# Splitting one memory value panel over four steps of an attention loop instead of two (one core)

## The reference, cut to what matters

```python
def memory_cross_attn(x, memn, wq, wkv, wo):
    B, S, _ = x.shape
    Mm = memn.shape[1]
    q = (x @ wq).reshape(B, S, XA_HEADS, XA_DH)
    k, v = jnp.split(memn @ wkv, 2, axis=-1)
    k = k.reshape(B, Mm, XA_HEADS, XA_DH)
    v = v.reshape(B, Mm, XA_HEADS, XA_DH)
    s = jnp.einsum('bshd,bmhd->bhsm', q, k).astype(jnp.float32) * (XA_DH ** -0.5)
    p = jax.nn.softmax(s, axis=-1)
    o = jnp.einsum('bhsm,bmhd->bshd', p.astype(v.dtype), v).reshape(B, S, XA_HEADS * XA_DH)
    return o @ wo
```

## Time and profile before

| | |
|---|---|
| median of 3 runs | 1854.23 us (1853.72 to 1860.33) |
| profiled execution | 1850.81 us |
| its span, first to last instruction | 1849.0 us |
| mean granted TensorE clock | 0.981 |
| busy: PE, DVE, ACT, POOL | 96%, 57%, 20%, 10% |
| first attention steps of the change, layer 0 | from 904 us |
| the same, layer 1 | from 1431 us |

### The profile page before, as it was taken

The page is one execution under the profiler, slowest core; times in us unless marked ns, Lnnn a source line. Parts: engine busy times, 40 slices in busy tenths (PEclk is TensorE's granted clock), DMA queues, the critical chain, the costliest instruction groups (busy, mean ns, idle before and its releaser), DMA issues.

```text
span 1849.0 us, 22062 instructions
## 1 busy us (share of the span) xinstructions
PE 1768.0 (96%) x8510; PEld 1303.6 (71%) x8510; DVE 1052.9 (57%) x2078; ACT 361.3 (20%) x885; POOL 190.8 (10%) x126
## 2 busy tenths in 40 slices
PE   7999999989899999999999999999999999999997
PEld 6886488644746886476785759994668776689953
DVE  6776565343654777561163048996812451369985
ACT  1111000140511111102261112220012340222210
POOL 1212111000020222111000100002110000000010
PEclk9999999989999999999989999999999899999999
DMA  9644364521164545346412525543455205164440
GB/s 327 198 147 172 115 223 137 203 69 68 47 200 149 178 166 182 114 136 177 168 47 83 178 71 180 183 160 136 156 140 187 89 1 188 63 200 154 171 159 23
DMA packets 162502, 265.59 MB, mean 144 GB/s; under 512 B 4008, under 2 KB 105684, under 8 KB 162270
## 3 DMA queue, kind: packets, MB, share of 16 engines
q1 hardware_dynamic: 157470, 248.18, 39.9%
q0 software_dynamic: 4768, 15.48, 2.5%
q10 hardware_dynamic: 160, 0.52, 0.1%
HBM read 262.56 MB, written 1.08 MB: 143 GB/s over the span
## 4 chain that ended last, share of the span: by engine, by line
PE 75%; DVE 15%; DVEq 4%; ACT 3%; issue 2%; DMA 1%; SPq 0%; ACTq 0%
PE psum L764 14%; PE psum L924 11%; PE psum L820 9%; PE psum L737 8%; PE psum L727 6%; PE psum L1042 4%; PE psum L1077 3%; PE psum L1303 3%; PE psum L1260 3%; PE psum L714 3%; DVE work L2296 3%; PE psum L975 2%; PE psum L876 2%; DVE ring L1813 2%; PE psum L862 2%
## 5 line engine op out<-in xcount | busy, mean ns | idle before, releaser
L608 POOL TENSOR_TENSOR work<-ring,work 128x1024 f32<-128x1024 f32 (+1 forms) x57 | 141.4, 2481 | 803.9 <-DVE work L1815 803.9
L924 PE MATMUL psum<-ring,work 128*128 128x512 f32 x352 | 161.1, 593 | 2.7 <-DVE work L2329 2.7
L1811 DVE TENSOR_TENSOR work<-ring 128x1024 f32<-128x1024 f32 (+1 forms) x83 | 102.2, 1232 | 80.1 <-PE psum L924 77.7
L737 PE MATMUL psum<-ring,x_t 128*128 128x512 f32 x320 | 140.0, 595 | 7.4 <-ACT x_t L1361 7.4
L924 PEld LDWEIGHTS psum<-ring,work 128*128 128x128 f32 x352 | 66.3, 190 | 84.3 <-issue 79.9
L924 PE MATMUL psum<-work 128*128 128x512 f32 x264 | 122.6, 593 | 0.1
L737 PEld LDWEIGHTS psum<-ring,x_t 128*128 128x128 f32 x320 | 60.0, 190 | 81.5 <-issue 71.8
L1955 DVE CUSTOM_DVE_ANT_0 work<-psum,work 128x256 f32<-128x256 f32 (+1 forms) x96 | 31.4, 364 | 140.6 <-PE psum L1042 140.5
L1813 DVE TENSOR_TENSOR ring<-ring 128x1024 f32<-128x1024 f32 (+1 forms) x83 | 102.3, 1232 | 6.2
L1815 DVE TENSOR_TENSOR work<-ring 128x1024 f32<-128x1024 f32 (+1 forms) x83 | 99.6, 1200 | 6.5 <-issue 0.4
L1042 PE MATMUL psum<-work 128*128 128x256 f32 (+2 forms) x416 | 90.0, 351 | 3.9 <-ACT work L1596 2.2
(11 more groups left out here) (253 smaller groups left out, 2933.5 us busy)
## 6 DMA issues: line engine op xcount, KB each, us to landing
ring<-in_ffn_w_up_dram SPq DMA_DIRECT2D x66, 1024.0 KB, 8.0
ring<-in_w_in_dram SPq DMA_DIRECT2D x21, 2048.0 KB, 7.9
ring<-in_ffn_w_down_dram SPq DMA_DIRECT2D x20, 2048.0 KB, 7.8
ring<-in_ffn_w_gate_dram SPq DMA_DIRECT2D x22, 1024.0 KB, 5.5
ring<-in_xa_wkv_dram SPq DMA_DIRECT2D x8, 2048.0 KB, 8.0
ring<-in_w_out_dram SPq DMA_DIRECT2D x6, 2048.0 KB, 8.7
ring<-in_xa_wq_dram SPq DMA_DIRECT2D x4, 2048.0 KB, 7.8
ring<-in_xa_wo_dram SPq DMA_DIRECT2D x4, 2048.0 KB, 9.5
```

The lines of the kernel that those rows point to most:

```text
L608: nc.gpsimd.tensor_tensor(t4, quarters(n, chunks, pitch)[2], t2, ALU.subtract).then_inc(fourth_ready, 1)
L737: return mm(bank(banks[2 * i + h]), acts[:, c, i * P:(i + 1) * P], ring[:, (n0 + c // 4) % RING, o:o + 512], start=(c == 0), stop=(c == KD ...
L924: last = mm(sums[p], acts[p][:, q, :], rhs[:, i, :], start=(q == 0), stop=(q == KF // 2 - 1))
L1811: v.tensor_tensor(t3, b22, b12, ALU.subtract)
```

## The change

The tile function gets a range of chunks. Each of four steps, 1 to 4, now computes one piece: tile 0 chunks 0 to 3, tile 0 chunks 4 to 7, tile 1 chunks 0 to 3, tile 1 chunks 4 to 7. The wait for the memory keys stays at step 1, now ahead of the first piece; the wait for the panel's arrival moves there too. `panel_done` is incremented behind the fourth piece. ACT copies at its step 5 instead of 4.

```diff
-                def memory_values(j, tiles, banks):
+                def memory_values(j, tiles, banks, chunks=range(KD)):
 
                     n = at(L_WV[j], N_LAYER, l)
-                    if 0 in tiles:
+                    if 0 in tiles and 0 in chunks:
                         arrived(n)
                     for i in tiles:
-                        for k in range(KD):
+                        for k in chunks:
                             last = mm(bank(banks[i]), MEMT[:, k, i * P:(i + 1) * P], ring[:, n % RING, k * 512:k * 512 + 512],
                                       start=(k == 0), stop=(k == KD - 1))
-                    if 1 in tiles:
+                    if 1 in tiles and KD - 1 in chunks:
                         last.then_inc(panel_done, 1)
 
-                def keys_out():
-                    pe.wait_ge(group_free, at(H_WK + 2, G_LAYER, l))
-
-                def first_values():
-                    memory_values(0, (0,), (1, 3))
-
-                def second_values():
-                    memory_values(0, (1,), (1, 3))
+                def values_between(i, half):
+
+                    def between():
+                        if (i, half) == (0, 0):
+                            pe.wait_ge(group_free, at(H_WK + 2, G_LAYER, l))
+                        memory_values(0, (i,), (1, 3), range(4 * half, 4 * half + 4))
+                    return between
...
-                attend(UNITS_2, U1, l, {1: keys_out, 2: first_values, 3: second_values})
+                attend(UNITS_2, U1, l, {1 + 2 * i + h: values_between(i, h) for i in range(TT) for h in range(2)})
...
-                attend(UNITS_2, U1, l, {4: lambda: memory_values(0, (1, 3), 2)})
+                attend(UNITS_2, U1, l, {5: lambda: memory_values(0, (1, 3), 2)})
```

## The result

| | before | after |
|---|---|---|
| median | 1857.57 us (7 runs, 1853.72 to 1860.35) | 1841.80 us (7 runs, 1839.93 to 1849.69) |
| ratio | | 0.9922, 95% interval 0.9902 to 0.9942 |
| profiled execution, span | 1849.0 us | 1838.1 us |
| mean granted clock | 0.981 | 0.987 |

The ratio means 14.5 us less (10.8 to 18.2).

What follows compares the result with a forecast made beforehand. Bound by a chain of matmuls (75% PE), partly at low clock. Layer gains of 7.5 and 7.1 us make 14.6, cut to 12.2: 1854.23 - 12.2 = 1842.0 us (chance 0.58), range 1836.2 to 1844.6; 8 in 10 up to 1850.5.

Steps and rivals of the forecast that it cites:

- first fall: Per layer, TensorE's clock drops to 1.2 GHz during the K scores; the first half product behind them loses 3.2 us.
- thin work: Matmuls with 15 columns or 15 rows, said to stand before all four clock falls, with PE busy at the first.
- second fall: Per layer, low clock behind turn, value(0) and the hole; costs 3.6 us: value(1) 1.7, turn(2) 0.2, later units 1.7.
- hole: PE idle 0.77 us before turn(2), during ACT's copy of the second K unit's turned probabilities; 0.8 us per layer.
- The sum to scores(5): PE time from the first K scores to scores(5) if the clock stays up: 24.9 us, against 30.7 before in layer 0.
- The stretch: From the first K scores to scores(14), where 256-key units start: 37.9 us per layer, against 45.4 and 45.0 before.
- Small moves: Earlier panel use, key wait, later ACT copies, product switches: each taken as 0; copies bounded at 1.0 us per layer.
- From 14.6 to 12.2: Both layers' gain, 14.6 us if every fall goes, lowered to 12.2 since low stretches may be shorter; bounds 9.6 to 14.6.
- Rival A: One fall stays behind scores(3), turn(1), value(0), slowing the fourth piece: gain 7.2 us for both layers, 1847.0 us; chance 0.27.
- Rival B: Both falls stay, only shifted, and just the hole goes: gain 1.6 us, 1852.6 us; chance 0.10.
- Rival C: A fall behind each of four thin stretches per layer: 10.4 us slower for two layers, 1864.6 us; chance 0.05.

Runs made afterwards that it cites:

- Run 10: The changed kernel with only one chunk of the first value tile between the two K scores, the other seven at step 2: 1845.60 us, ratio 0.9948.
- run 5: The kernel before with four chunks of the first value tile computed once more between the two K scores, result unused: 1853.56 us, ratio 0.9997.
- Run 1: The kernel before with only the first value tile split, over steps 1 and 2; second tile whole at step 3: 1846.39 us, ratio 0.9956.
- run 3: The kernel before with only ACT's two value copies moved from step 4 to step 5: 1853.37 us, ratio 0.9992.
- Run 2: The kernel before with only the second value tile split, over steps 3 and 4, and ACT's copies at step 5: 1846.21 us, ratio 0.9957.
- run 4: The changed kernel with ACT's copies back at step 4 instead of 5: 1841.59 us, ratio 0.9928.
- run 8: The changed kernel with the second tile in three pieces at steps 3, 4 and 5, copies at step 6: 1840.26 us, ratio 0.9921.
- run 11: The changed kernel with the fourth piece halved over steps 4 and 5, copies at step 6: 1840.65 us, ratio 0.9919.

## Why the prediction was right

- **The price of the first fall** (3.2 us per layer): right for a low stretch of 6.8 us. Run 10 has such a fall in one layer and not in the other, 3.3 us apart, and run 5 buys 3.6 us of extra work with it. Run 1 takes it alone away and its stretch is 3.0 us shorter. With a low stretch of 3.4 us, as in run 3, it costs half.
- **Its cause**, thin work: run 5 leaves neither idle time nor transfers as the cause of the first fall. What it is in the thin products that lets the clock fall, no run shows: their 15 columns, their 64 rows and the weight loads that filled 3.20 of 3.20 us there (PEld in the earlier trace rows) were never parted.
- **The second fall and the hole** (3.6 + 0.8): right in sum. Run 2 removes both and gives 8.0 us for two layers, as expected. No run takes the hole away and leaves the fall, so their shares rest on rows alone, and whether the hole helps to bring the fall about is open. It can't be all of it: in layer 1 of before the clock, read in steps of 0.2 us, falls at 1457.1, when PE has only just gone idle (the scores ahead of the hole end at 1456.26 + 0.71 = 1456.97). The hole itself I read as 0.77 us of idle PE from the chain; PE's timeline has 0.60.
- **The sum to scores(5)**, 24.9 us: measured 932.23 - 906.99 = 25.2. Two errors nearly cancel. Three of four pieces took 3.63 us instead of 3.43: the switches, which I took at 0 from one row, cost 0.2 each. The K scores took 1.88 instead of 2.00, since I had halved a row of 4.00 us whose last 0.8 us ran at the low level.
- **The stretch**, 37.9 us: measured 38.4 and 38.3, 0.4 to 0.5 over, 0.3 of it ahead of scores(5). Behind that the 1.52 us per unit were right.
- **Small moves**: right where a run tests them. The copies stand at 931.77 to 932.8, before DVE has finished `output(1)` and begun logits(5) at 933.47, and runs 3 and 4 show no price. The arrival of the panel and the wait for the keys left no gap in front of the first piece.

```profile
931.77 1.05 ACT L1618 COPY work<-psum 128x512 f32<-128x512 f32 x2
...
933.47 0.28 DVE L1954 CUSTOM_DVE_ANT_0 work<-psum,work 128x128 f32<-128x128 f32 x1
```

- **From 14.6 to 12.2**: the reason was right, since run 3 shows the cheaper fall that I had assumed as the lower bound (1.5 us measured, 1.6 assumed), and the same order gave gains of 11.9, 13.4 and 14.5 us in three measurements. The 1842.0 against 1841.8 measured is luck: before came out at 1857.57 over seven runs instead of 1854.23 (3.3 more), and the medians lie 15.8 us apart instead of 12.2 (3.6 more; by the ratio the gain is 14.5), and the two cancel.
- **Rival A** put a remaining fall at scores(3), turn(1), `value(0)`. None of the profiles of the change's order shows one there. One remains in layer 1, a place further on, and is free, because DVE sets the pace of the loop there. I had scaled a fall's price by its length only, and not by where it lands.
- **Rival B** is excluded by the interval. The Trainium skill, "TensorE: Matmul & The Clock Gate", section "HAM oscillation — how this bites in real kernels", looks for the cause in idle gaps of PE. The trace doesn't agree for the first fall: PE was busy 3.20 of 3.20 us ahead of it, and run 5 removed it without any gap being closed.
- **Rival C** is excluded too: of the four thin stretches of after only `value(1)` is followed by a fall, and only in layer 1. The Trainium skill, same page, section "A second HAM failure mode: psum-queue depth-cycling", tells of a kernel that cycles through PSUM banks and in which PE idles for short times between its groups of matmuls often enough for the clock to go up and down. The prediction left out the idling. Here PE goes from group to group without a gap (busy 26.00 of 26.00 us from 1427 on), and runs 8 and 11, which change oftener than the change, show no fall in the stretch; so the section's case isn't tested, and what the runs show is that alternation without idling does no harm.

## What to carry to other kernels

Look at the granted clock by stretch before counting instructions: in this kernel it fell while PE was busy with matmuls of few columns or few rows, and the dense product behind them paid. Dense work that has to be done anyway can then be put between the thin matmuls instead of behind them; here four chunks (3.4 us) between two K scores were enough in every layer profiled, and one chunk wasn't. Judge such an edit by a stretch of the profile as well as by the time, because falls elsewhere move single executions by several microseconds, and look at several profiles, because a fall of one and the same order can be half as long in the next.

## What was not expected of the hardware

- Extra matmuls can be free where they keep the clock up: 6.9 us of added product changed the time by -0.6 us (-3.2 to +1.9).
- A fall has no fixed price: 3.2 us where 6.8 us at the low level hit dense products (before), 1.5 us where it was 3.4 us (run 3, the same order on PE), and nothing measurable where DVE sets the pace (after, layer 1).
- A piece of 8 records behind K scores or behind a 15-row value took 3.63 us in the chain, behind a turn 3.44. No run shows why.
